# Hybrid decoder block on one core: the first range's modulation product shared between TensorE and VectorE, with single-pass fillers on TensorE

## What is computed

```python
c_act = jax.nn.silu(c)                       # (1, 2048)
mod = c_act @ ada_w[l] + ada_b[l]            # (1, 2048) @ (2048, 12288)
sh1, sc1, g1, sh2, sc2, g2 = split(mod, 6)
u = rms_norm(x, mix_norm_pre[l]) * (1.0 + sc1) + sh1
y = token_mixer(u, w_in[l], ...)             # begins with u @ w_in, 2048 x 16384
```

## Time and profile before

| | |
|---|---|
| median of 3 runs | 1848.81 us (1842.44 to 1849.19) |
| profiled execution, first to last instruction | 1846.5 us |
| median less that span | 2.3 us |
| TensorE busy | 1820.6 us, 99% |
| VectorE busy | 1348.9 us, 73% |
| ScalarE busy | 874.8 us, 47% |
| mean granted TensorE clock | 0.996 |

### The profile page before, as it was taken

How to read it: one execution, slowest core, us unless ns; L and a number is a source line. 1 busy time by engine, 2 the same in 40 slices (tenths; PEclk the granted TensorE clock), 3 DMA queues, 4 the chain that set the end, 5 groups by cost and what they waited for, 6 DMA issues and landing times.

```text
span 1846.5 us, 26480 instructions
## 1 busy us (share of the span) xinstructions
PE 1820.6 (99%) x9108; PEld 1542.0 (84%) x9108; DVE 1348.9 (73%) x1923; ACT 874.8 (47%) x1056; POOL 189.5 (10%) x269
## 2 busy tenths in 40 slices
PE   6999999999999999999999999999999999999998
PEld 4888888888888888888888878888888888888886
DVE  4788788978777777788887667777777777755555
ACT  4544454445364545464445555444444444444444
POOL 0000022222222222222220000000000000000000
PEclk8999999999999999999999999999999999999999
DMA  9899788878878787878885646555655555555552
GB/s 354 297 347 388 226 264 263 281 247 259 282 244 276 247 280 247 280 239 292 285 273 183 232 133 195 193 182 189 195 184 184 194 190 182 185 202 189 197 189 107
DMA packets 274964, 432.78 MB, mean 234 GB/s; under 512 B 21060, under 2 KB 144660, under 8 KB 274256
## 3 DMA queue, kind: packets, MB, share of 16 engines
q1 hardware_dynamic: 244304, 360.77, 59.3%
q0 software_dynamic: 20736, 67.34, 10.5%
q10 hardware_dynamic: 9856, 3.76, 0.8%
HBM read 429.69 MB, written 2.13 MB: 234 GB/s over the span
## 4 chain that ended last, share of the span: by engine, by line
PE 97%; DVE 1%; ACT 1%; DMA 0%; issue 0%; SPq 0%; DVEq 0%; ACTq 0%
PE ps L936 17%; PE ps L562 12%; PE ps L564 12%; PE ps L563 12%; PE ps L593 10%; PE ps L944 9%; PE ps L1004 4%; PE ps L1003 4%; PE ps L1002 4%; PE ps L694 2%; PE ps L695 1%; PE ps L696 1%; PE ps L601 1%; PE ps L663 1%; PE ps L643 1%; DMA x_sb<-in_x 0%
## 5 line engine op out<-in xcount | busy, mean ns | idle before, releaser
L1449 DVE TENSOR_TENSOR w_low<-stage,w_high 128x1024 fp32r<-128x1024 f32 x608 | 743.9, 1224 | 414.6 <-ACT w_high L1048 393.0
L1048 ACT ACTIVATE w_high<-stage 128x1024 fp32r<-128x1024 f32 x552 | 583.9, 1060 | 720.3 <-PE ps L564 281.5
L562 PE MATMUL ps<-w_high,lhs 128*128 128x512 f32 x992 | 391.2, 394 | 0.0
L564 PE MATMUL ps<-w_high,lhs 128*128 128x512 f32 x992 | 386.8, 390 | 0.0
L563 PE MATMUL ps<-w_low,lhs 128*128 128x512 f32 x992 | 386.1, 389 | 0.0
L936 PE MATMUL ps<-lhs,w_high 128*128 128x512 f32 x1408 | 336.7, 391 | 0.6 <-DVE lhs L1488 0.6
L936 PEld LDWEIGHTS ps<-lhs,w_high 128*128 128x128 f32 x1408 | 258.5, 188 | 50.7 <-DVE lhs L1488 0.8
L546 POOL DMA_DIRECT2D ada_ring<-in_ada_w x256 | 185.0, 723 | 773.7 <-DVE ada_acc L1475 540.1
L1475 DVE SCALAR_TENSOR_TENSOR ada_acc<-ada_ring,c_act,ada_acc 128x256 f32<-128x256 f32 x480 | 231.0, 481 | 17.2 <-DMA ada_ring<-in_ada_w 7.0
L564 PEld LDWEIGHTS ps<-w_high,lhs 128*128 128x128 f32 x992 | 186.2, 188 | 39.7
L563 PEld LDWEIGHTS ps<-w_low,lhs 128*128 128x128 f32 x992 | 186.4, 188 | 37.0
(11 more groups left out here) (208 smaller groups left out, 1516.9 us busy)
## 6 DMA issues: line engine op xcount, KB each, us to landing
stage<-in_w_in SPq DMA_DIRECT2D x100, 1024.0 KB, 6.6
stage<-in_ffn_w_up SPq DMA_DIRECT2D x176, 512.0 KB, 4.3
ada_ring<-in_ada_w POOLq DMA_DIRECT2D x256, 256.0 KB, 5.5
stage<-in_ffn_w_down SPq DMA_DIRECT2D x44, 1024.0 KB, 5.0
ada_first<-in_ada_w SPq DMA_DIRECT2D x64, 512.0 KB, 10.9
stage<-in_w_in SPq DMA_DIRECT2D x56, 512.0 KB, 11.4
stage<-in_ret_w_o SPq DMA_DIRECT2D x16, 1024.0 KB, 6.3
stage<-in_moba_w_o SPq DMA_DIRECT2D x16, 1024.0 KB, 6.6
```

What stands on the lines that cost most here:

```text
L562: pe.matmul(acc, hi, w_high[:, slot, k, :], start=kt == 0, stop=False)
L564: last = pe.matmul(acc, lo, w_high[:, slot, k, :], start=False, stop=kt == KT - 1)
L1048: act.activation(w_high[:, h % 4, :, :], stage[:, slot, 2 * (h % 2):2 * (h % 2) + 2, :], ACT.Copy).then_inc(high_ready, 1)
L1449: dve.tensor_tensor(w_low[:, h % 4, :, :], stage[:, slot, 2 * (h % 2):2 * (h % 2) + 2, :], w_high[:, h % 4, :, :].bitcast(F32), ALU.subtra ...
```

## The change

In range 0 every slot is now shared: VectorE takes the first k tile of each megabyte (8 steps in place of 14), and TensorE the second (`opening_sums`, 8 matmuls of one moving column for each slot, 64 in all in place of 16). TensorE works on a slot when it lands, and the turning of `x` is cut in four and put between the slots. The fillers become one matmul of fp32r operands, on a constant column block: `ones_r`, now written at the start, and the last k tile of `lhs`, set to 1.0 by VectorE. There are 24 before the first slot, then 4, 2, 2 and 2, then 4 before each of the slots 4 to 7, 1 before the sum over partitions and 9 behind it. The loads of slots 4 to 7 of range 0, and the first four of range 1, wait for both engines. Of range 0's four k tiles of `u` the odd ones are made by VectorE (`first_u_odd`), the even ones by ScalarE. On VectorE the shift, scale and odd tiles of range 0 are made ahead of the low part of piece 1, and the first step of range 1 behind the low parts of `lhs`.

```diff
         def ada_steps(st):
-            return KT - ada_rows(st)
+            return KT - ada_rows(st) if st else ada_slots(0)
         def direct_slot(st):
-            return ada_slots(st) - (4 if st else 2)
+            return ada_slots(st) - 4
         def ada_row(st, i):
+            if st == 0:
+                return ada_rows(0) * i
...
-                    if slot_ == direct_slot(st_):
-                        sp.wait_ge(ada1_direct, st_ + 1)
+                    if st_ == 0:
+                        sp.wait_ge(ada1_direct, slot_ + 1)
+                    if st_ and slot_ == direct_slot(st_):
+                        sp.wait_ge(ada1_direct, directs_through(st_))
                     else:
                         sp.wait_ge(ada1_step, steps_through(st_, slot_))
...
             pe.wait_ge(ones_set, 1)
+            pe.wait_ge(cols_ready, 2)
+            pe.wait_ge(warm_set, 2)
...
                 for _ in range(times):
-                    pe.matmul(ps[:, 7, :], ident[:, :], x_sb[:, 0, 0:NC], start=True, stop=True)
+                    pe.matmul(ps[:, 7, :], ones_r[:, :], lhs[:, KT - 1, :], start=True, stop=True)
+
+            def opening_sums(slot):
+                pe.wait_ge(ada1_in[slot % 4], 32 * (slot // 4 + 1))
+                width = 4 * len(FIRST_PAIRS[0])
+                for i in range(width):
+                    at = (width + i) * P
+                    last = pe.matmul(ps[:, 6, i:i + 1], ada_first[:, slot % 4, at:at + P],
+                                     c_act[:, 2 * slot + 1:2 * slot + 2], start=slot == 0 and i == 0, stop=False)
+                last.then_inc(ada1_direct, 1)
...
-            turn_x()
+            keep_warm(24)
+            opening_sums(0)
+            keep_warm(4)
+            for slot in (1, 2, 3):
+                turn_x(2 * slot - 2, 2 * slot)
+                keep_warm(2)
+                opening_sums(slot)
+            turn_x(6, 8)
...
-            keep_warm(11)
-            direct_sums(0, 0, 16)
-            keep_warm(2)
+            for slot in range(4, ada_slots(0)):
+                keep_warm(4)
+                opening_sums(slot)
+            keep_warm(1)
             sum_first(0)
-            keep_warm(4)
+            keep_warm(9)
...
-                    for kt in (2 * pair, 2 * pair + 1):
+                    for kt in (2 * pair, 2 * pair + 1)[:2 if st else 1]:
                         act.activation(src_b[:, kt, :], src_a[:, kt, :], ACT.Identity, bias=shift1[:, kt:kt + 1],
                                        scale=scale1[:, kt:kt + 1]).then_inc(u_ready, 1)
...
+            dve.memset(lhs[:, KT - 1, :].bitcast(F32), 1.0).then_inc(warm_set, 1)
+            dve.wait_ge(ones_set, 1)
+            dve.tensor_copy(ones_r[:, :], ones[:, 0:1].broadcast_to([P, P])).then_inc(warm_set, 1)
             dve.wait_ge(cols_ready, 2)
...
+            def first_u_odd():
+                dve.wait_ge(scale1_ready, 1)
+                for pair in FIRST_PAIRS[0]:
+                    kt = 2 * pair + 1
+                    dve.wait_ge(xT_ready, pair + 1)
+                    dve.tensor_scalar(src_b[:, kt, :], src_a[:, kt, :], scale1[:, kt:kt + 1], shift1[:, kt:kt + 1],
+                                      ALU.mult, ALU.add).then_inc(u_odd_ready, 1)
...
+                if n == 1:
+                    first_shift_scale(0)
+                    first_u_odd()
...
-            dve.wait_ge(ones_set, 1)
-            dve.tensor_copy(ones_r[:, :], ones[:, 0:1].broadcast_to([P, P]))
```

More of the change, by code:

```diff
@@ L223, in hybrid_block @@
         ones_set = sem("ones_set")
+        warm_set = sem("warm_set")
         cols_turned = sem("cols_turned")
@@ L240, in hybrid_block @@
         u_ready = sem("u_ready")
+        u_odd_ready = sem("u_odd_ready")
         ada_in = [sem(f"ada_in{b}") for b in range(4)]
@@ L373, in ada_steps, with directs_through @@
         def ada_steps(st):
-            return KT - ada_rows(st)
+            return KT - ada_rows(st) if st else ada_slots(0)
         def direct_slot(st):
-            return ada_slots(st) - (4 if st else 2)
+            return ada_slots(st) - 4
         def ada_row(st, i):
+            if st == 0:
+                return ada_rows(0) * i
             return i if i < ada_rows(st) * direct_slot(st) else i + ada_rows(st)
         def steps_through(st, slot):
+            if st == 0:
+                return slot + 1
             return ada_steps_before(st) + ada_rows(st) * (slot + 1 if slot < direct_slot(st) else slot)
+        def directs_through(st):
+            return ada_slots(0) + st
         def ada_steps_before(st):
@@ L616, in _, with turn_x @@
             pe.transpose(ps[:, 4, 0:7 * KT], rows[:, :], ident[0:7 * KT, 0:7 * KT]).then_inc(cols_turned, 1)
-            def turn_x():
+            def turn_x(lo, hi):
                 pe.wait_ge(x_scaled, 2)
-                for pair in range(KT // 2):
+                for pair in range(lo, hi):
                     wait(pe, xT_ready, pair - 3)
@@ L1110, in first_u @@
                 for pair in FIRST_PAIRS[st]:
-                    for kt in (2 * pair, 2 * pair + 1):
+                    for kt in (2 * pair, 2 * pair + 1)[:2 if st else 1]:
                         act.activation(src_b[:, kt, :], src_a[:, kt, :], ACT.Identity, bias=shift1[:, kt:kt + 1],
                                        scale=scale1[:, kt:kt + 1]).then_inc(u_ready, 1)
-                    act.wait_ge(u_ready, 2 * pair + 2)
+                    if st:
+                        act.wait_ge(u_ready, 2 * pair + 2 - len(FIRST_PAIRS[0]))
+                    else:
+                        act.wait_ge(u_ready, pair + 1)
+                        act.wait_ge(u_odd_ready, pair + 1)
                     lhs_pair(0, pair, src_b, -1)
@@ L1550, in _ @@
                 next_st, steps = ada_ops_behind(n)
+                if n == 1:
+                    first_shift_scale(0)
+                    first_u_odd()
                 if st is not None:
[L1552 to L1555, removed]
+                    if st:
+                        first_shift_scale(st)
+                        if steps:
+                            first_ada(next_st, steps[0])
+                            steps = steps[1:]
                     for pair in FIRST_PAIRS[st]:
                         lhs_pair(0, pair, src_b)
+                    if st == 0:
+                        for i in ada_ops_behind(1)[1]:
+                            first_ada(1, i)
                 add_streamed(n)
                 low_part(n, n // 2 % 4, n)
-                for i in steps:
-                    first_ada(next_st, i)
+                if n != 1:
+                    for i in steps:
+                        first_ada(next_st, i)
             add_streamed(8 * G_FIRST)
-            dve.wait_ge(ones_set, 1)
-            dve.tensor_copy(ones_r[:, :], ones[:, 0:1].broadcast_to([P, P]))
             dve.wait_ge(consts_in, 48)
```

## The result

| | before | changed |
|---|---|---|
| median, 7 runs each | 1848.93 us | 1855.85 us |
| lowest to highest | 1842.44 to 1849.19 | 1852.5 to 1858.97 |
| profiled execution, first to last instruction | 1846.5 us | 1852.2 us |
| time of that execution | not given | 1854.31 us |
| mean granted clock | 0.996 | 0.991 |

The changed kernel is slower: the ratio is 1.0048, 95% interval 1.0035 to 1.0062. The forecast of 1848.0 was 8 us low; the time lies inside the range of 1840 to 1857.

What follows compares the result with a forecast made beforehand. TensorE was taken to bound the kernel (97% of the chain). From 1848.8 us, a 7.1 us gain at full clock was set against a clock fall among slots 4 to 7, about no change: 1848 us, range 1840 to 1857.

Steps and rivals of the forecast that it cites:

- I take them as done when slot 0 lands: Opening: the 24 first fillers were taken as finished when slot 0 lands, at 13.8 us.
- second rival: Opening: clock low from the first slots on, after the gap before slot 0; 1866 us, 1858 and up if it returns; chance 0.12.
- a low clock before slot 4: Opening, sign to check in the changed profile: a low clock before slot 4 would make the forecast wrong.
- a fall among slots 4 to 7: Opening, the forecast itself: clock falls among slots 4 to 7; 1848 us, own range 1844 to 1855, chance 0.45.
- the likeliest case: Opening: clock falls at the end of slot 5 (32.2 us); products start at 50.1 us, 0.9 later than before.
- The four places of the fall: Slots 4 to 7: start 0.9 us later for slot 5's end, -1.5 one slot later, 3.3 one earlier, 5.7 at slot 4.
- The fourth case: Opening: TensorE keeps up with the landings; products at 38.8 us, 10.4 earlier, 1838.4 us; chance 0.06.
- the path behind the sum: From the sum over partitions to the first product: 3.0 us, bounds 2.7 to 3.5, no change from before.
- full-clock plan of 42.1: Opening at 2.4 GHz throughout: sum ends at 39.1 us, products start at 42.1 against 49.2, 7.1 us earlier.
- a tie: Loads of slots 4 to 7, now also waiting for TensorE: 0 us, 1 us at worst if the last slot is late.
- The rival that the gain is given back: Range 1: a load or the step on it is late and products wait; about 1848.8 us; chance 0.05.
- The full-clock case at 42.1: Whole kernel, rival: clock holds throughout, products start 7.1 us earlier; 1841.7 us; chance 0.32.

Runs made afterwards that it cites:

- e1_bridge: Changed kernel with 32 in place of 24 first fillers, so TensorE does not stand still before slot 0 lands; 1851.17 us.
- e5_one_late: Changed kernel with TensorE's share cut to the last k tile of the last slot, VectorE taking the other fifteen, 45 fillers before it; 1843.86 us.
- e8_later: e5_one_late with 21 in place of 13 fillers after the sum; 1842.68 us.
- e2_dense: e1_bridge with 8 in place of 4 fillers before each of slots 4 to 7; 1848.21 us.
- e3_no_fill: e1_bridge with no fillers before slots 4 to 7; 1846.71 us.
- e6_old_order: e5_one_late with ScalarE making all four k tiles of u and piece 1's low part ahead of shift and scale; 1842.87 us.
- e9_no_direct: e5_one_late with VectorE taking all 16 k tiles, 56 fillers before the sum and 24 after; 1842.99 us.
- e4_mixed: e1_bridge with the 4 fillers of each of slots 4 to 7 put one by one between its one-column matmuls; 1851.12 us.

## Why the prediction was wrong

**The step that failed** first is "I take them as done when slot 0 lands", of the 24 first fillers. The prediction had the clock's rise inside them near 12 to 14 us and took the pause as nothing. They ended at 12.1, the pause was 1.67 us, the clock fell at 14.7, and the small vectors were turned at 30.8 in place of 27.2: 3.6 us. In e1_bridge eight fillers closed the pause and the fall was gone; the same stretch then took 13.6 us where the prediction had 13.4. The prediction had named the gap before slot 0 as the place of its second rival, and a low clock before slot 4 as a sign of being wrong; both came.

**The second failed step** is how the cases were set beside each other. A fall at the first slots and a fall among slots 4 to 7 stood as two rivals, one at 1866 and one at 1848. They came together: the first was short, the clock was back at 21.6, and the second fell as forecast. From the likeliest case, with its fall in slot 5, 0.9 us later than before, plus 3.6, plus some 1.2 us for the half slot by which the fall came sooner, one gets 5.7, nearly the 6.0 us measured. That the time lies inside the stated range is thus in part luck: with an early fall the prediction had priced 1858 us and up.

**Sums that don't hold.** The four places of the fall that are priced give -1.5, 0.9, 3.3 and 5.7 us, and their middle is 2.1 us later than before, 1850.9 us, not 1848. "The fourth case", twice, is the third of the list of rivals. And a measurement was taken to tell 9.2 us from no change; here the interval is under 3 us to either side, and 6.9 us stand clear of it.

**What was right.** The terms at full clock: a slot's matmuls 1.7 us (1.6 predicted), a period of slots 1 to 3 3.08 (3.1), the path behind the sum 2.95 (50.90 to 53.85, predicted 3.0), the two odd tiles 0.74 together (0.6). TensorE, not VectorE, set the end of the opening: VectorE's last step ended at 36.4, TensorE's last slot at 47.1. Beyond the 3.6 us before slot 4, the measured 55.2 differs from the full-clock plan of 42.1 in slots 4 to 7 (16.3 us, not 10.0), in filler and sum (3.8, not 1.9) and in the nine fillers (they ended at 54.9, 4.0 after the sum, where 3.0 were wanted).

**The loads of slots 4 to 7**, "a tie", were not: the late slots 0 to 3 held them back, the windows show 320 and 348 GB/s where 387 stood before, and VectorE took slot 7 at 35.1 in place of 32.8. As said, TensorE did not feel it.

**The rival that the gain is given back** had 0.05 and deserved more. The prediction counted 8.5 us of still queue as slack for a gain of 7.1. e5_one_late and e8_later show the limit at a start of some 43 us, 6 us before the old one. The full-clock case at 42.1 would by this have run into it, and no kernel here reached a median of 1841.7; the case itself was not run.

**The theory** that the loss is the clock's stands on e1_bridge (one fall less, 4.7 us less), e2_dense (16 fillers more, no fall, faster) and the mean clock of every run: the changed kernel's fastest run had 0.992, its slowest 0.989. But the clock is not all of it. With the fillers that it takes to hold the clock, the shared scheme starts at 47.8, 7.4 us sooner than the changed kernel; leaving the modulation to VectorE starts at 43, another 4.8 sooner. VectorE alone keeps up: its steps on a megabyte take 2 x 1.28 us, and one lands every 2.71. The 64 one-column matmuls, 1.7 us per slot with fillers to pay for them, put TensorE into a path where VectorE had been in time. The prediction saw TensorE as the new bound, yet held that against a gain of 7.1 us, which came from comparing with an old opening that had itself lost its clock; its faster runs take 1842.7 us, as the kernels that start at 43 do (that these kept the clock is read from their mean clock alone).

The Trainium skill, "TensorE: Matmul & The Clock Gate", section "Why this matters for your kernels", warns of idle gaps between bursts. The first fall did follow a gap, though one of 1.67 us, shorter than those that the Trainium skill names there, and it was gone when the gap was closed (e1_bridge). The second is not told by it: at 35.2 us TensorE had been issuing without a pause since 13.8, and in e3_no_fill at 30.3 as well. The Trainium skill, same page, section "Part 4: PE-mode transpose", says that transposes don't count as busy for the clock gate in the same way. e1_bridge speaks against it: its clock held through slots 1 to 3 with 0.8 us of turning and 0.55 of fillers beside each 1.7 of one-column work, and fell among slots 4 to 7 with 1.0 of fillers and no turning.

**Best version.** e8_later, e6_old_order and e9_no_direct lie within 0.3 us of each other and beat both kernels (ratios to before of 0.998, intervals under 1). They are no faster than the kernel before in its good runs (1842.6 to 1842.9): what they bring is that most runs are good ones, 24 of the 32 under 1843.2 us. Whether another order of loads would make an earlier start worth something was not tried.

## What to carry to other kernels

Before moving small matmuls onto TensorE because it looks idle, look at what else it must do by the same deadline and whether the engine that had the work was late at all; here VectorE was within 2.6 us of the last landing. Too few fillers cost twice, for themselves and at the low clock: compare none, some and enough. And a start that is moved forward should be followed to the next thing that waits for a transfer; a start earlier than that can use brings nothing, and time wasted up to it is free, as e8_later shows.

## What was not expected of the hardware

- The clock falls under continuous issue: 1.7 us of one-column float32 matmuls in every 2.7 us brought it down (34.0 us in e1_bridge), also with the fillers mixed in between (e4_mixed, 32.2 us).
- One kernel, the same program, has its runs in two groups 6 us apart (1842.7 and 1848.8) with mean clocks of 0.999 and 0.995 or 0.996. The gap fits the 14 us of low clock that the traced run of the slower group has from 34.4 us on; a run of the faster group was not traced.
- In e5_one_late pauses of 1.7 and 0.3 us at the sums for ranges 1 and 3 were each followed by a fall of 3.4 us, in the midst of dense products. The same sums without a pause (e8_later) had none.
